# The first attention tiles: small tables for tile 0, masked corners in device memory, earlier key transposes, and the split in front of the reciprocal multiply

## The chip, the cores and the metric

The kernel runs on one core of a Trainium2 chip. The metric is the time of one execution on the device in microseconds (us). TensorE (PE) multiplies matrices and transposes, VectorE (DVE), ScalarE (ACT) and GpSimd (POOL) do the elementwise work, and SyncE (SP) issues nearly all DMAs. Each engine works through its own list of instructions in order; semaphores order the engines among each other.

## The reference

One layer for 1024 prompt frames and 64 sample frames, width 1024. A combined projection gives two attention branches, gates and indexer values. Branch A keeps the best 256 keys per query (by an indexer) and attends over these; branch B attends over the own chunk of 64 and the two before. Both normalise queries and keys by head and add a relative-position bias.

```python
logits = einsum('nqcgd,nqkcd->nqcgk', qg, ks) * HEAD_DIM ** -0.5 + bias    # A; only selected, admissible keys
probs  = softmax(where(valid, logits, NEG))
p      = exp(logits - m); o = einsum(p, v) / (p.sum() + exp(sink - m))     # B; window of whole chunks, sinks
o_a = (att_a * silu(z_a)) @ w_oa ; o_b = (att_b * silu(z_b)) @ w_ob
y   = x + gate * ((sigmoid(g_a) * o_a + sigmoid(g_b) * o_b) @ w_out)
```

A key is admissible if its chunk of 64 is not later than the query's. So in the diagonal block of 128 by 128 the first 64 queries must not see the last 64 keys: one masked corner per tile. Outputs are also the normalised keys, the values and the updated caches.

## The kernel before

The tokens are nine tiles: 0 to 7 of 128 prompt frames, 8 the sample. The kernel has four stages: (1) modulation, norm and transposes of x; (2) projection in 99 pieces (NP), each a product over eight blocks of the contraction in three fp32r matmuls, while VectorE selects the top keys and writes MASK (0 or 1e30); (3) attention; (4) the two output products. The projected q, k and v go to device memory (snat), as do the gates (gz).

Attention is a list of units: per tile eight heads of branch A, then eight of branch B, so 16 units (steps s) a tile; each engine has a loop over s with its own offsets. Per unit u, TensorE computes the negated logits (L1870; for A also a small matmul that adds MASK, L1874), VectorE adds the negated bias and takes the row minimum (L1550), ScalarE takes the exponential (L1255), TensorE transposes the probabilities (L1806), VectorE or ScalarE copies them out of PSUM (t_evac, L544 and L549), and TensorE multiplies with the values (L1896). The biases are tables laid out in device memory by then (btad for A, btbd for B, 128 x 8 heads x keys). Tile 0 has a table of its own for A (BT0) and values for A (VA0). VectorE writes 1e30 into two corners of BTB at s = 6 (L1517, L1518), after the loads of BTB and VB.

The next tile is prepared meanwhile. SP loads QKV at step 16(tt-1) - 7 (L787). POOL multiplies by the norm's weights (L964) and by the reciprocal root (L972) at - 5, and at SPLIT_AT splits q and k into a high and a low part (L981 to L993). TensorE transposes the queries at steps + 9 to + 12 and the keys at + 13 and + 14 (L1829, Q and K in TP). The keys of the sample's cache take the same way in between: ScalarE and POOL split one block of them at steps 32, 48, ... (KSC, L1278, L1009), and TensorE transposes it six steps later.

The end of a group g (a branch of a tile) takes four steps. VectorE multiplies the result with the gate (L1533; the gate is loaded by SP into ATS, L795). The reciprocals of the sums are transposed and go to device memory and back as a broadcast (rdd, RB: L800, L808). POOL multiplies with them (L1004, eight steps after the group's end), and SP stores it (attd, L828). There are two buffers ATS, so a gate load waits for the store of the group two before. SP's list runs in the order of s: gate load, reciprocals, and for the next tile QKV come behind the store of the group before.

## Time and profile before

| | us |
|---|---|
| runs, median of 3 (lowest to highest) | 1006.3 (1005.08 to 1006.81) |
| profiled execution, span from first to last instruction | 1006.1 |
| PE busy | 954.1 (95%) |
| DVE busy | 662.4 (66%) |
| ACT busy | 395.6 (39%) |
| POOL busy | 371.7 (37%) |

The profiled execution shows no time of its own beside the span. Attention runs from about 562 to 803 us of the span, tile 1 from 582.9, tile 2 from 602.2. A row of a timeline has the start, the duration, engine, line, operation, what is written from what, and in brackets how long the engine stood idle before and what ended it.

### The profile page before, as it was taken

The numbers are of one execution on the slowest core, as the hardware profiler recorded it, in microseconds if no ns is written. First come the engines' busy times: TensorE is split into PE (matmuls) and PEld (weight loads), VectorE is DVE, ScalarE is ACT, GpSimd is POOL, SyncE is SP. The second block draws the span as 40 slices with busy tenths as digits, with TensorE's granted clock in tenths as the row PEclk, the third lists the DMA queues.
The fourth block names the chain that finished last, engine by engine and source line by source line (L and its number), as shares of the span: only waits on it lengthen the run. The fifth ranks groups of instructions, "written<-read, shape, count | busy, mean of one in ns | idle before, by whom it ended". The sixth has DMA issues, their size and how long they took to land.

```text
span 1006.1 us, 17578 instructions
## 1 busy us (share of the span) xinstructions
PE 954.1 (95%) x6441; PEld 851.9 (85%) x6455; DVE 662.4 (66%) x1378; ACT 395.6 (39%) x1175; POOL 371.7 (37%) x417
## 2 busy tenths in 40 slices
PE   4859999999999999999999898999999899999998
PEld 2558887878789999999999776787778599999998
DVE  6563365999999999999981475766665763431121
ACT  5674566444432322121211465676665632212100
POOL 0261113212242533131224386766640135536342
PEclk9989999999999999999999789999999999999999
DMA  9830013643462323232231844333315655524342
GB/s 326 304 78 25 24 37 107 226 166 94 127 218 66 108 76 115 74 112 79 66 136 49 254 119 130 118 120 109 106 47 158 194 154 177 161 74 153 110 131 75
DMA packets 110907, 125.87 MB, mean 125 GB/s; under 512 B 10969, under 2 KB 88153, under 8 KB 110698
## 3 DMA queue, kind: packets, MB, share of 16 engines
q1 hardware_dynamic: 100418, 113.77, 36.3%
q10 hardware_dynamic: 10408, 11.01, 3.6%
q8 instruction: 52, 0.85, 0.4%
q14 instruction: 29, 0.24, 0.1%
HBM read 94.96 MB, written 35.75 MB: 130 GB/s over the span
## 4 chain that ended last, share of the span: by engine, by line
PE 82%; issue 4%; DMA 4%; POOL 3%; DVE 3%; ACT 3%; SPq 1%; ACTq 0%; POOLq 0%; DVEq 0%
PE PS L1623 20%; PE PS L1625 19%; PE PS L1624 19%; PE PS L1870 6%; PE PS L1896 6%; PE PS L1806 4%; PE PS L1720 2%; PE PS L1829 2%; POOL YO L1035 1%; PE PS L1874 1%; PE PS L1684 1%; DMA out_y_prompt<-YO 1%; DMA XN<-in_x_prompt 1%; PE PS L1632 1%; DMA VB<-snat 1%
## 5 line engine op out<-in xcount | busy, mean ns | idle before, releaser
L1623 PE MATMUL PS<-HH,WH 128*128 128x384 f32 (+1 forms) x576 | 188.8, 328 | 0.0
L1625 PE MATMUL PS<-HH,WL 128*128 128x384 f32 (+1 forms) x576 | 187.9, 326 | 0.0
L1624 PE MATMUL PS<-HL,WH 128*128 128x384 f32 (+1 forms) x576 | 187.7, 326 | 0.0
L1449 DVE MAX8 M<-SC 128x8 f32<-128x384 f32 (+3 forms) x210 | 174.8, 870 | 11.6 <-DVE SC L1454 11.0
L1454 DVE MATCH_REPLACE8 SC<-M,SC 128x384 f32<-128x384 f32 (+3 forms) x210 | 179.9, 863 | 0.0
L908 POOL TENSOR_TENSOR WL<-RAW,WH 128x512 fp32r<-128x512 f32 x72 | 94.0, 1310 | 180.9 <-ACT WH L1054 180.9
L1623 PE MATMUL PS<-WH,HH 128*128 128x512 f32 (+3 forms) x288 | 110.1, 382 | 8.8 <-DVE HL L1393 8.7
L1623 PEld LDWEIGHTS PS<-HH,WH 128*128 128x128 f32 x576 | 108.1, 188 | 3.8 <-issue 3.7
L1624 PE MATMUL PS<-WL,HH 128*128 128x512 f32 (+3 forms) x288 | 108.4, 376 | 0.0
L1625 PE MATMUL PS<-WH,HL 128*128 128x512 f32 (+3 forms) x288 | 108.2, 376 | 0.0
L1624 PEld LDWEIGHTS PS<-HL,WH 128*128 128x128 f32 x576 | 108.1, 188 | 0.0
L1625 PEld LDWEIGHTS PS<-HH,WL 128*128 128x128 f32 x576 | 108.1, 188 | 0.0
L1255 ACT ACTIVATE PB<-PB,NM 128x256 f32<-128x256 f32 (+9 forms) x136 | 86.2, 634 | 24.1 <-DVE NM L1550 23.1
L1181 ACT ACTIVATE STG<-PS 128x384 f32<-128x384 f32 (+1 forms) x48 | 22.7, 474 | 155.2 <-PE PS L1625 155.2
L1623 PE MATMUL PS<-UH,MH 128*128 128x256 f32 x256 | 72.6, 283 | 0.0
L1624 PE MATMUL PS<-UL,MH 128*128 128x256 f32 x256 | 72.5, 283 | 0.0
L1625 PE MATMUL PS<-UH,ML 128*128 128x256 f32 x256 | 72.3, 282 | 0.0
L1623 PEld LDWEIGHTS PS<-WH,HH 128*128 128x128 f32 (+1 forms) x288 | 53.8, 187 | 19.9 <-POOL WL L908 8.8
L1550 DVE CUSTOM_DVE_ANT_0 PB<-PS,BTA 128x256 f32<-128x256 f32 (+6 forms) x56 | 46.1, 823 | 33.9 <-PE PS L1874 22.3
L1806 PE MATMUL PS<-IDF,PB 128*128 128x128 f32 (+1 forms) x436 | 66.1, 280 | 0.8 <-ACT PT L549 0.7
L1623 PE MATMUL PS<-ZH,WOH 128*128 128x384 f32 (+1 forms) x192 | 63.3, 330 | 1.9 <-POOL WOL L1021 1.9
L1625 PE MATMUL PS<-ZH,WOL 128*128 128x384 f32 (+1 forms) x192 | 63.0, 328 | 0.0
(216 smaller groups left out, 1939.9 us busy)
## 6 DMA issues: line engine op xcount, KB each, us to landing
RAW<-in_w_all SPq DMA_DIRECT2D x72, 256.0 KB, 2.7
gz<-STG SPq DMA_DIRECT2D x48, 192.0 KB, 1.8
WADA<-in_w_ada SPq DMA_DIRECT2D x16, 512.0 KB, 11.8
snat<-STG SPq DMA_DIRECT2D x24, 256.0 KB, 2.0
QKV<-snat SPq DMA_DIRECT2D x8, 768.0 KB, 4.8
GT<-gz SPq DMA_DIRECT2D x32, 192.0 KB, 2.5
XN<-in_x_prompt SPq DMA_DIRECT2D x8, 512.0 KB, 6.2
btad<-bvd ACTq DMA_DIRECT2D x4, 1024.0 KB
```

Source lines behind the costliest of these rows:

```text
L908: nc.gpsimd.tensor_tensor(WL[c % 2][:, k, 0:cw], raw, WH[c % 2][:, k, 0:cw].bitcast(F32), ALU.subtract).then_inc(lo_done, 1)
L1181: nc.scalar.activation(STG[:, q % 3, 0:gn], bank(pbank(p))[:, 0:gn], ACT.Sigmoid).then_inc(piece_ev, 1)
L1255: nc.scalar.activation(PB[u % NPB][0:r, 0:nk], PB[u % NPB][0:r, 0:nk], ACT.Exp, scale=-1.0, bias=NM[0:r, br, h:h + 1], accum_out=DEN[0:r, ...
L1449: V.max(M8[0:r, a, :], w).then_inc(sel_step, 1)
L1454: V.match_replace(w, M8[0:r, a, :], w, TAKEN).then_inc(sel_step, 1)
L1550: V.tensor_tensor_reduce(out=PB[u % NPB][0:r, 0:nk], in0=v, in1=bias, scale=1.0, scalar=init, op0=ALU.add, op1=ALU.min, accum_out=NM[0:r, ...
L1623: T.matmul(out, wh, mh, start=first, stop=False)
L1624: T.matmul(out, wh, ml, start=False, stop=False)
L1625: return T.matmul(out, wl, mh, start=False, stop=last)
L1806: last = T.transpose(out[0:m, c:c + r], PB[v % NPB][0:r, 128 * b:128 * b + m], IDF[0:r, 0:r])
L1870: last = T.matmul(out, q, keys[:, kv, part, k0 + b:k0 + b + m], start=(part == 0), stop=(part == 1 and br == 1))
L1896: last = T.matmul(PS[half, 7, 128 * h:128 * h + r], v, PT[PSLOT[u + kv] % 3][0:m, p_col(u + kv, b):p_col(u + kv, b) + r], start=(b == 0), ...
```

## The change

Tile 0 gets tables of its own for branch B too (BB0, VB0), loaded with BT0 during the last projection chunk. POOL fills a tile NEGT with 1e30, and SP stores it into the masked corners of btad and btbd in device memory, so tables loaded later have it; VectorE's two writes into BTB go, and tiles 0 and 1 leave the MASK matmul out. The K transposes of tile 0 go between the halves of the last projection piece; their copies out of PSUM wait for its end, since the key tables lie over the activations that it reads. The big tables are loaded in another order with semaphores of their own, and the sample's caches (CK, VAS, VBS) at step 14. Constants for the sample are prepared before the last selection. SPLIT_AT goes from 2 to 0: in POOL's loop the split stands before the reciprocal multiply and the cache keys' low part of the same step. Small edits not shown: buffer PB 4 changes places with the later ones, semaphores of the last stage are shared, two waits are added ahead of loads or writes into reused space.

```diff
+        SINKP = at("SINKP", [128, 4], F32, XB + 22784)
+        NSINKP = at("NSINKP", [128, 4], F32, XB + 22816)
         BT0 = at("BT0", [128, 8, 128], F32, WB + 65536)
         VA0 = at("VA0", [128, 128], F32, SCB + 18432)
+        VB0 = at("VB0", [128, 128], F32, SCB + 17920)
+        BB0 = [at(f"BB0{i}", [128, 4, 128], F32, SCB + 10240 + 4096 * i) for i in range(2)]
+        NEGT = at("NEGT", [128, 8, CHUNK], F32, XB + 18432)
         KTB = at("KTB", [128, 2, 2, SEQ], F32R, 102400)
...
-        assert all(TQ[n][1] == ("Q", 0, n) for n in range(EARLY_T))
+        EARLY_T = 6
+        assert [x for _, x in TQ[:EARLY_T]] == [("Q", 0, n) for n in range(4)] + [("K", 0, n) for n in range(2)]
         PREP0 = {16 * (tt - 1): tt for tt in range(NT)}
         CACHE_STEP = {16 * (2 + i): i for i in range(5)}
-        LOAD_AT, NORM_AT, SPLIT_AT = -7, -5, 2
+        LOAD_AT, NORM_AT, SPLIT_AT = -7, -5, 0
         RD_AT, FIN_AT = ({GEND[g] + d: g for g in range(2 * NT)} for d in (1, 4))
...
+                elif x[1] == 0:
+                    eng.wait_ge(piece_pe, NP)
+                    dst = (KTB if x[2] else KTA)[:, :, :, tcols(0)]
...
                         sp.dma_start(dst, src).then_inc(copy_out, 16)
+                if c == NCH - 1 and j == 1:
+                    sp.wait_ge(bias_out, 16 * 5)
+                    sp.wait_ge(neg_set, 1)
+                    sp.dma_start(btad[0:CHUNK, :, 960:1024], NEGT[0:CHUNK, :, :]).then_inc(neg_out, 16)
+                    sp.dma_start(btbd[0:CHUNK, :, 192:256], NEGT[0:CHUNK, :, :]).then_inc(neg_out, 16)
+                    sp.dma_start(btbd[CHUNK:128, :, 0:64], NEGT[CHUNK:128, :, :]).then_inc(neg_out, 16)
                 if c == NCH - 1 and j == 9:
-                    sp.wait_ge(bias_out, 16 * 5)
+                    sp.wait_ge(neg_out, 48)
                     sp.wait_ge(lo_done, KD * NCH)
                     sp.dma_start(BT0[:], btad[:, :, 896:1024]).then_inc(kva_in, 16)
                     sp.wait_ge(mask_done, NT)
                     sp.dma_start(VA0[:], snat[0:128, 640:768]).then_inc(kva_in, 16)
+                    for i in range(2):
+                        sp.dma_start(BB0[i][:], btbd[:, 4 * i:4 * i + 4, 128:256]).then_inc(kva_in, 16)
+                    sp.dma_start(VB0[:], snat[0:128, 1408:1536]).then_inc(vb0_in, 16)
                 if c == NCH - 1 and j == 8:
                     sp.wait_ge(xn4_ready, 1)
...
 
-            sp.dma_start(BTB[:], btbd).then_inc(kvb_in, 16)
-            sp.dma_start(VB[:], vp[:, :, 1408:1536]).then_inc(kvb_in, 16)
-            sp.dma_start(BTA[:, :, 768:1024], btad[:, :, 768:1024]).then_inc(kvc_in, 16)
-            sp.dma_start(VA[:], vp[:, :, 640:768]).then_inc(kvc_in, 16)
-            for dst, src in ((CK[:, 0:4, :], t["cache_ak"].rearrange("(n p) c -> p n c", p=128)), (CK[:, 4, :], t["cache_bk"]),
-                             (VAS[:, 0:4, :], t["cache_av"].rearrange("(n p) c -> p n c", p=128)),
-                             (VAS[0:DEC, 4, :], snat[SEQ:TOK, 640:768]),
-                             (VBS[:, 0, :], t["cache_bv"]), (VBS[0:DEC, 1, :], snat[SEQ:TOK, 1408:1536])):
-                sp.dma_start(dst, src).then_inc(rest_in, 16)
+            sp.dma_start(BTA[:, :, 768:1024], btad[:, :, 768:1024]).then_inc(bta_in, 16)
+            sp.dma_start(VA[:], vp[:, :, 640:768]).then_inc(va_in, 16)
+            sp.dma_start(BTB[:], btbd).then_inc(btb_in, 16)
+            sp.dma_start(VB[:], vp[:, :, 1408:1536]).then_inc(vb_in, 16)
             for i in range(3):
...
                     sp.dma_start(QKV[0:rows_of(tt), tt % 2, :], snat[tcols(tt), :]).then_inc(qkv_in[tt % 2], 16)
+                if s == 14:
+                    for dst, src in ((CK[:, 0:4, :], t["cache_ak"].rearrange("(n p) c -> p n c", p=128)), (CK[:, 4, :], t["cache_bk"]),
+                                     (VAS[:, 0:4, :], t["cache_av"].rearrange("(n p) c -> p n c", p=128)),
+                                     (VAS[0:DEC, 4, :], snat[SEQ:TOK, 640:768]),
+                                     (VBS[:, 0, :], t["cache_bv"]), (VBS[0:DEC, 1, :], snat[SEQ:TOK, 1408:1536])):
+                        sp.dma_start(dst, src).then_inc(rest_in, 16)
                 if s in ZT_AT:
                     g = ZT_AT[s]
...
+            nc.gpsimd.memset(NEGT[:], NEG_BIG).then_inc(neg_set, 1)
             pool.wait_ge(rms_ready, 1)
...
+                    act.wait_ge(pv_pe, 8)
                 if s == NU:
...
+            for i in range(2):
+                V.tensor_copy(IDP[:, i, :], IDF[0:DEC, 0:DEC])
+                half = slice(DEC * i, DEC * (i + 1))
+                V.tensor_copy(SINKP[half, :], SINK[half, :].rearrange("p (a b) -> p a b", b=2)[:, :, i])
+                link(V.tensor_scalar(NSINKP[half, :], SINK[half, :].rearrange("p (a b) -> p a b", b=2)[:, :, i], -1.0, None, ALU.mult))
...
-                    dve.wait_ge(kva_in, 32)
-                    for i in range(3):
+                    dve.wait_ge(kva_in, 64)
+                    for i in range(2):
                         dve.wait_ge(stg_out[i], 16 * NST[i])
                     dve.wait_ge(mask_done, NT)
-                if s == 6:
-                    dve.wait_ge(kvb_in, 32)
-
-                    for i in range(2):
-                        V.tensor_copy(IDP[:, i, :], IDF[0:DEC, 0:DEC])
-                        half = slice(DEC * i, DEC * (i + 1))
-                        V.tensor_copy(SINKP[half, :], SINK[half, :].rearrange("p (a b) -> p a b", b=2)[:, :, i])
-                        V.tensor_scalar(NSINKP[half, :], SINK[half, :].rearrange("p (a b) -> p a b", b=2)[:, :, i], -1.0, None, ALU.mult)
-                    V.memset(BTB[0:CHUNK, :, 192:256], NEG_BIG)
-                    link(V.memset(BTB[CHUNK:128, :, 0:64], NEG_BIG))
-                if s == 16:
-                    dve.wait_ge(kvc_in, 32)
-                if s % 16 == 0 and 32 <= s < U8:
-                    dve.wait_ge(bta_in, 16 * (s // 16 - 1))
+                if s == 4:
+                    dve.wait_ge(stg_out[2], 16 * NST[2])
+                if s == 24:
+                    dve.wait_ge(btb_in, 16)
+                if s % 16 == 0 and 16 <= s < U8:
+                    dve.wait_ge(bta_in, 16 * (s // 16))
                 if s == U8:
                     dve.wait_ge(btp_in[0], 32)
...
+                        bias = BTBP[:, h, :] if tt == SAMPLE else BTB[:, h, j0:j0 + nk] if tt else BB0[h // 4][:, h % 4, :]
                         init = (NSINKP if tt == SAMPLE else NSINK)[:, h:h + 1]
                     dve.wait_ge(qk_pe, u + 1)
...
-                piece(p)
+                if p == NP - 1:
+                    piece(p, (0, 1))
+                    for n in (4, 5):
+                        transposes(TQ[n][1])
+                    piece(p, (2, 3))
+                else:
+                    piece(p)
                 if p in GATE_AT:
                     ada_gate(GATE_AT[p])
                 for n in {NP - 4: (0, 1), NP - 2: (2, 3)}.get(p, ()):
                     transposes(TQ[n][1])
 
-            pe.wait_ge(piece_ev, NP)
             pe.wait_ge(mask_done, NT)
             for s in range(S0, S1):
-                if s == 0:
-                    pe.wait_ge(kva_in, 32)
-                if s == 8:
-                    pe.wait_ge(kvb_in, 32)
-                if s == 16:
-                    pe.wait_ge(kvc_in, 32)
+                if s < 2 and s >= 0:
+                    pe.wait_ge(piece_ev, NP - 2 * (1 - s))
+                if s == 5:
+                    pe.wait_ge(kva_in, 64)
+                if s == 13:
+                    pe.wait_ge(vb0_in, 16)
+                if s == 21:
+                    pe.wait_ge(va_in, 16)
+                if s == 29:
+                    pe.wait_ge(vb_in, 16)
                 if s == 32:
                     pe.wait_ge(rest_in, 96)
                 if 0 <= s < NU:
@@ -1868,8 +1895,8 @@
                         out = PS[:, 2 * (u % 2) + b // 512, 0:m]
                         for part in range(2):
                             last = T.matmul(out, q, keys[:, kv, part, k0 + b:k0 + b + m],
-                                            start=(part == 0), stop=(part == 1 and br == 1))
-                        if br == 0:
+                                            start=(part == 0), stop=(part == 1 and (br == 1 or tt < 2)))
+                        if br == 0 and tt >= 2:
                             r = rows_of(tt)
                             last = T.matmul(out, ident, MASK[0:r, MOFF[tt] + b:MOFF[tt] + b + m], start=False, stop=True)
...
-                                v = VBS[0:m, b, half] if tt == SAMPLE else VB[0:m, max(tt - 1, 0) + b, half]
+                                v = VBS[0:m, b, half] if tt == SAMPLE else VB[0:m, tt - 1 + b, half] if tt else VB0[:, half]
                             last = T.matmul(PS[half, 7, 128 * h:128 * h + r], v, PT[PSLOT[u + kv] % 3][0:m, p_col(u + kv, b):p_col(u + kv, b) + r],
```

## Rows read from the trace of the kernel before

**Rows 1.** The page, part 4: the chain that ended last, by engine.
```profile
PE 82%; issue 4%; DMA 4%; POOL 3%; DVE 3%; ACT 3%; SPq 1%; ACTq 0%; POOLq 0%; DVEq 0%
```
**Rows 2.** Stretches: each engine's busy us (instructions), TensorE's granted clock, DMA share, GB/s.
```profile
564.00:568.00 4.00, 3.85 (x22) 3.20 (x21) 1.62 (x9) 2.38 (x12) 3.92 (x6) 0.55 1.05 350
568.00:572.00 4.00, 1.84 (x11) 1.31 (x10) 3.04 (x12) 1.15 (x5) 1.50 (x4) 0.50 1.11 325
...
620.00:624.00 4.00, 4.00 (x34) 3.53 (x33) 2.46 (x7) 2.27 (x7) 3.23 (x4) 0.70 0.34 96
...
664.00:668.00 4.00, 4.00 (x43) 3.36 (x43) 2.67 (x7) 2.81 (x6) 2.82 (x3) 1.00 0.62 224
```
**Rows 3.** Timeline of TensorE, tiles 0 and 1: start, us, operation, idle before and releaser.
```profile
560.82 0.89 PE L1829 MATMUL PS<-IDR,KS 128*128 128x128 f32 x8 [0.53 <-ACT STG L1181]
...
571.34 0.66 PE L1870 MATMUL PS<-KTB,QT 128*128 128x128 f32 x2 [2.06 <-DVE NM L1550]
...
586.22 0.28 PE L1874 MATMUL PS<-MASK,IDB 128*128 128x256 bf16 x1
```
**Rows 4.** Timeline of ScalarE after the last projection piece.
```profile
560.67 0.58 ACT L558 CAST QT<-PS 128x512 fp32r<-128x512 f32 x1
561.75 0.59 ACT L581 CAST KTB<-PS 128x512 fp32r<-128x512 f32 x1 [0.50 <-PE PS L1829]
```
**Rows 5.** Timeline of VectorE, tiles 0 and 1.
```profile
568.02 0.29 DVE L1513 CAST IDP<-IDF 64x64 bf16<-64x64 f32 x1 [1.59 <-DMA VB<-snat]
...
570.89 0.29 DVE L1550 CUSTOM_DVE_ANT_0 PB<-PS,BT 128x128 f32<-128x128 f32 x1
...
597.58 0.69 DVE L1533 TENSOR_TENSOR ATS<-PS,ATS 128x512 f32<-128x512 f32 x1
```
**Rows 6.** Timeline of SP's DMA issues: start, us spent issuing, line, tiles.
```profile
561.16 0.43 SPq L746 DMA_DIRECT2D BTB<-btbd  x1
...
573.54 0.50 SPq L787 DMA_DIRECT2D QKV<-snat  x1
...
585.43 0.39 SPq L828 DMA_DIRECT2D attd<-ATS  x1
...
587.77 0.36 SPq L795 DMA_DIRECT2D ATS<-gz  x1
...
592.67 0.58 SPq L787 DMA_DIRECT2D QKV<-snat  x1
```
**Rows 7.** Timeline of POOL, tile 2's preparation and the start of tile 3's.
```profile
578.42 3.34 POOL L964 TENSOR_TENSOR XG<-QKV,GAM 128x512 f32<-128x512 f32 x4 [8.92 <-DMA QKV<-snat]
...
584.13 1.28 POOL L1004 TENSOR_TENSOR ATS<-ATS,RB 128x512 f32<-128x512 f32 x1
585.36 1.05 POOL L981 TENSOR_TENSOR QS<-XG,RYQ 128x512 fp32r<-128x512 f32 x1
...
591.38 1.71 POOL L993 TENSOR_TENSOR KS<-XNB,KS 128x128 fp32r<-128x128 f32 x4
...
597.25 3.35 POOL L964 TENSOR_TENSOR XG<-QKV,GAM 128x512 f32<-128x512 f32 x4 [0.45 <-DMA QKV<-snat]
...
608.77 0.88 POOL L1009 TENSOR_TENSOR KSC<-CK,KSC 128x128 fp32r<-128x128 f32 x2
```
**Rows 8.** Timeline of TensorE: transposes of cache keys (KSC), first of tile 3's queries (QS).
```profile
611.13 0.53 PE L1829 MATMUL PS<-IDR,KSC 128*128 128x128 f32 x4
...
617.46 0.51 PE L1829 MATMUL PS<-IDR,QS 128*128 128x128 f32 x4 [2.74 <-POOL KS L993]
...
638.35 0.54 PE L1829 MATMUL PS<-IDR,KSC 128*128 128x128 f32 x4
...
664.44 0.54 PE L1829 MATMUL PS<-IDR,KSC 128*128 128x128 f32 x4
...
693.90 0.54 PE L1829 MATMUL PS<-IDR,KSC 128*128 128x128 f32 x4
```
**Rows 9.** DMA issues by line: count, KB of one, median us from issue to landing.
```profile
ATS<-gz SPq DMA_DIRECT2D x16, 256.0 KB, 3.0
```

More of the change, by code:

```diff
@@ L172, in build_program @@
         BTBP = at("BTBP", [128, 4, WIN + DEC], F32, 121856)
-        IDP = at("IDP", [DEC, 2, DEC], BF16, 66560)
-        SINKP = at("SINKP", [128, 4], F32, 66816)
-        NSINKP = at("NSINKP", [128, 4], F32, 66848)
+        IDP = at("IDP", [DEC, 2, DEC], BF16, XB + 22528)
+        SINKP = at("SINKP", [128, 4], F32, XB + 22784)
+        NSINKP = at("NSINKP", [128, 4], F32, XB + 22816)
         BT0 = at("BT0", [128, 8, 128], F32, WB + 65536)
         VA0 = at("VA0", [128, 128], F32, SCB + 18432)
+        VB0 = at("VB0", [128, 128], F32, SCB + 17920)
+        BB0 = [at(f"BB0{i}", [128, 4, 128], F32, SCB + 10240 + 4096 * i) for i in range(2)]
+        NEGT = at("NEGT", [128, 8, CHUNK], F32, XB + 18432)
         KTB = at("KTB", [128, 2, 2, SEQ], F32R, 102400)
@@ L292, in build_program @@
         stg_out = [sem(f"stg_out{i}") for i in range(3)]
+        neg_set = sem("neg_set")
+        neg_out = sem("neg_out")
         kva_in = sem("kva_in")
-        kvb_in = sem("kvb_in")
-        kvc_in = sem("kvc_in")
+        vb0_in = sem("vb0_in")
+        va_in = sem("va_in")
+        btb_in = sem("btb_in")
+        vb_in = sem("vb_in")
         rest_in = sem("rest_in")
@@ L342, in build_program @@
         u_lo = sem("u_lo")
-        xr_in = [sem(f"xr_in{i}") for i in range(3)]
         y_pe = sem("y_pe")
@@ L348, in build_program @@
         y_up = sem("y_up")
-        y_out = [sem(f"y_out{i}") for i in range(3)]
         SOFF = {}
@@ L777, in _ @@
                     sp.wait_ge(exp_done, NU)
+                    sp.wait_ge(sink_sum, NT)
                     g_load(0)
@@ L1543, in _ @@
                         j0 = 128 if tt == 0 else 0
-                        bias = BTBP[:, h, :] if tt == SAMPLE else BTB[:, h, j0:j0 + nk]
+                        bias = BTBP[:, h, :] if tt == SAMPLE else BTB[:, h, j0:j0 + nk] if tt else BB0[h // 4][:, h % 4, :]
                         init = (NSINKP if tt == SAMPLE else NSINK)[:, h:h + 1]
```

13 lines of the change are left out of this document (6 added, 7 removed).

## The prediction

> **What bounds the kernel now.** I read the page first: TensorE holds 82% of the chain that ended last [rows 1]. So the kernel is bound by TensorE except where TensorE stands still, and the question is where it does. The view of stretches shows two such places near the change. At the start of attention (564 to 572 us) the granted clock falls to 0.55 and 0.50, the lower level of 1.2 GHz, and TensorE is busy for 1.84 of 4 us in the second stretch; around 620 it falls again, to 0.70 of a stretch's mean [rows 2]. From 664 on the stretches are full (4.00 of 4.00). So what is lost before about 664 us stays lost to the end, and what is gained there is kept only if nothing else holds TensorE up before 664.
>
> The timelines by engine say who holds it. At 571.34 TensorE has been idle for 2.06 us for a row minimum of VectorE (NM L1550) [rows 3]; VectorE had stood 1.59 us for the load of VB and then did nine small instructions (IDP, SINKP, NSINKP, two corners of BTB) [rows 5]. The second place is 617.46: 2.74 us for POOL's split of tile 3 (KS L993) [rows 8]. Both are what the change goes for.
>
> The order that matters is a ring through POOL and SP. Per tile, SP stores the attention output of group 0 (attd, L828) only after POOL's reciprocal multiply (ATS L1004); the next gate load (ATS, L795) waits for that store; then come the store and reload of the reciprocals, and only then the next tile's QKV load (L787). In the trace: multiply starts 584.13 and lasts 1.28, store 585.43, gate load 587.77, QKV load 592.67, POOL starts on it at 597.25 [rows 6, 7]. SP follows POOL here to 0.02 us, so the multiply's end sets all of it.
>
> **The change part by part.** All sums are against the profiled span, 1006.1 us; the runs shown have a median of 1006.3, 0.2 more, so nothing of note lies around the span.
>
> *First keys sooner.* The eight K transposes of tile 0 (0.89 us at 560.82) move into the last projection piece. They lengthen that piece by 0.64 to 0.72 (an estimate: their own 0.89 less the pipelined tail), so its end, its evacuation and the four big loads behind it on SP come 0.7 later. What was waited for behind them stays: ScalarE does the evacuation of the piece, then QT (0.58), then KTB (0.59) [rows 4], one after the other, and unit 0 needs KTB. Before, the transposes lay beside QT. From the later end, 0.44 + 0.58 + 0.59 less some overlap gives unit 0 at about 562.6 against 562.5. Bounds: 0.9 gained if the transposes' whole row vanished, 0.7 lost if nothing did. I take 0.
>
> *Small early tables, corners in memory, constants earlier.* The VB wait (1.59) and the nine instructions (568.02 to 570.9) leave VectorE [rows 5]. The six that prepare IDP and SINKP go ahead of the last selection rounds, far from TensorE's needs; the corners become one POOL memset and three stores during the last projection chunk, some 25 us before they are needed. The 256 KB x2 and 64 KB loads go out with BT0 beside the projection. If that cover failed, unit 0 would wait by the length of a load, 3 to 4 us; I put it at nothing. The removed stall is worth TensorE's idle 2.06 at least and VectorE's 4.4 at most. Next late is TensorE itself, full at the half clock, so I take 2.1.
>
> *Masks left out in tiles 0 and 1.* Sixteen small matmuls go (0.28 us for one of 256 columns [rows 3]). Bounds: nothing, where VectorE is waited for, and 16 x 0.28 = 4.5. They are pipelined and the next matmul starts about 0.12 behind one, so I take 1.4. The lead is then 2.1 + 1.4 = 3.5 us by unit 25 (bounds 0 to 9).
>
> *Load order.* Ahead of tile 2's QKV load SP now issues BTA, VA, BTB and VB (3072 KB as before), while CK, VAS and VBS (704 KB by their shapes) go behind it. Before, the first table was issued at 561.16, SP got to the QKV load at 573.54 and POOL started at 578.42 [rows 6, 7]. The DMAs move 325 to 350 GB/s in these stretches [rows 2], so 0.72 MB less is 2.2 us sooner; the later end of the last piece takes back 0.7. POOL starts on tile 2 at 578.4 - 2.2 + 0.7 = 576.9. Bounds: 579.1 (only the delay) and 572.0: SP itself reaches this load 5.5 us sooner, and if it landed as soon after its issue as before it would be 572.9, less at most 1. I take 576.9, because that data still queues behind the same 3 MB.
> The Trainium skill (DMA: Bandwidth & Descriptors, Anatomy of one DMA) fits a transfer at 2.0 us plus bytes over 436 GB/s, a fit made for POOL's own queue. By it the 4.26 MB up to this load would take 11.8 us from 561.9, an estimate of 573.7, and the final sum below would be 3.2 smaller; the 325 to 350 GB/s of the trace do not bear out that rate, and the sum goes without it.
>
> *Split ahead of the reciprocal multiply.* This is the part that decides. The split moves from step 2 to step 0 of each 16, and in POOL's loop the split stands before the multiply of the same step and before the cache keys' low part (KSC L1009). So multiply and KSC now queue behind 7.73 us of split (585.36 to 593.09, the last row's end) [rows 7]. Who waits for the multiply: SP's store at the next step, and behind it the gate load, the reciprocals of group 1 and the next QKV load. Who waits for KSC: TensorE's transposes of the cache keys at step 38, in program order three steps before tile 3's own query transposes.
>
> The ring before: end of multiply to QKV issue 592.67 - 585.41 = 7.26; to POOL's start 4.58; the two norm steps 5.71 (578.42 to 584.13); multiply 1.28; together 18.9 us, with the split beside SP's part. After: the split is inside, 18.9 + 7.73 = 26.6 us per tile. TensorE needs, from cache transposes to cache transposes, 27.2 for the first turn (of which 2.74 idle, and about 1 at a lower clock), 26.1 for the second and 29.5 for the third [rows 8]. So a ring that had some 5 us of air per tile now has none until tile 4 or 5.
>
> In absolute times. First multiply ends at 576.9 + 5.71 + 7.73 + 1.28 = 591.6 (before 585.4).
> - Gate load of group 2 goes at 591.6 + 2.36 = 594.0 and lands 3.0 later (median of that load [rows 9]), 597.0. VectorE needs it for the multiply that it did at 597.58 [rows 5]. With the lead of 3.5 it would be there at 594; so it waits 3 us and the lead is gone.
> - Second multiply ends at 591.6 + 26.6 = 618.2, KSC 0.88 later [rows 7], 619.1. The cache transposes were at 611.13: 8.0 us late.
> - Third: 618.2 + 26.6 = 644.8, KSC 645.7; before 638.35: 7.3 late. TensorE by itself would come at 619.1 + 23.4 = 642.5, some 1.5 more with the half clock after the long idle, so it waits again.
> - Fourth: 671.4, KSC 672.3; before 664.44: 7.9 late. TensorE by itself: 645.7 + 26.1 = 671.8.
> - Fifth: 698.9 against 672.3 + 29.5 = 701.8 by TensorE itself. From here TensorE is the bound, and the delay stays.
>
> So the sum is not the lead minus something; the lead is swallowed, and the ring sets +7.9. I add 0.8 for later QKV loads that may land slower beside other traffic and for half clock after the two short waits (0 to 2). +8.7 on 1006.1 is 1014.8, 1015.0 beside the median of the runs.
>
> **The rivals.**
> 1. *The ring does not bind, and the lead is kept* (not slower). Place: POOL's start on tile 2. All later times go with it one to one, so at 576.9 - 7.9 = 569.0 the fourth KSC is on time. Then the lead of 3.5 and perhaps the 2.74 at 617.46 stay won: 1000 to 1003. For it: SP is free for this load near 568 and the split of tile 3 did stand 4 us behind a multiply that waited for its data. Against: the load itself would have to land a microsecond after its issue, behind 3 MB. Or SP's chain from multiply to QKV load would have to shrink from 7.3 us, which is made of waits for DMAs that the change leaves in place. Chance 0.10.
> 2. *Lead and ring cancel.* POOL starts on tile 2 at 569 to 571, or the ring is 2 to 3 us shorter a turn: 1004 to 1008. For it the same rows as rival 1; against it that both ends of the load's bounds lie above 571. Chance 0.08, of which 0.05 within 0.2%.
> 3. *Worse: the waits cost the clock as well.* TensorE stands about 8 us ahead of the first cache transposes; after the 2.74 us at 617 the trace shows a lower clock (0.70) for one stretch [rows 2, 8]. If each of the three waits costs 1.5 to 2 us more, and QKV loads land 2 us later, the end is 1018 to 1022. Chance 0.10.
> The forecast itself has 0.72, with its own range from 1010.5 (load at the 573 bound, ring 26) to 1018.
>
> **How the numbers follow.** A difference under 0.2%, 2 us, cannot be told from no change here. Slower: forecast, rival 3 and a rest of rival 2, 0.72 + 0.10 + 0.01 = 0.83; same 0.05; faster 0.10 + 0.02 = 0.12. The range of 8 in 10 leaves out rival 1 and the far end of rival 3: 1008 to 1019.5.
>
> **What would show it.** In the changed trace: VectorE without the 4.4 us near step 6, and unit 8 about 2 us sooner; unit 0 within 0.3 of 562.5; POOL on tile 2 at 575 to 578, its first L1004 behind the split, ending near 591.6; SP's first attd store there and not at 585; VectorE's second L1533 no sooner than 597; TensorE idle for several us ahead of the KSC transposes, near 619; steps of about 26.6 us between the L1004 that follow splits; the granted clock low behind these waits. I am wrong if the first L1004 behind the split ends before 586, or if the KSC transposes run at 611 or sooner, or if TensorE still waits for KS L993 and not for KSC.

## The result, and the profile after the change

The changed kernel takes 1021.57 us (median of 4 runs, 1020.52 to 1023.54), the kernel before 1005.72 beside it: ratio 1.0162, 95% interval 1.0144 to 1.0181. The change costs 1.6%. The forecast had the sign and the place right (slower, through the ring of POOL and SP) and the size too small: 1015.0, with a range that ended at 1019.5.

In the profiled execution the span is 1020.3 us, against 1006.1. The device time of that execution is 1022.09, 1.8 above its span, and it is 1.8 to 2.0 above the span in every run since. If it was so for the kernel before too, its profiled execution took some 1007.9 (an estimate, its time is not on record), about 2 more than the median of its own kernel. The prediction had put 0.2 there.

The page's chain of work that ended last has a new member:

```profile
PE 77%; POOL 8%; issue 5%; DMA 3%; DVE 3%; ACT 2%; SPq 1%; ACTq 0%; POOLq 0%; DVEq 0%
```

POOL holds 8% of it where it held 3% [rows 1], TensorE 77% where it held 82%. The stretches say where (columns as in [rows 2]: busy us of PE, PEld, DVE, ACT, POOL; granted clock; DMA share; GB/s):

```profile
564.00:568.00 4.00, 3.39 (x17) 2.59 (x18) 1.85 (x13) 3.09 (x14) 3.67 (x6) 0.66 0.92 261
568.00:572.00 4.00, 3.77 (x23) 3.06 (x22) 1.76 (x10) 1.93 (x8) 0.00 (x0) 0.50 1.06 371
616.00:620.00 4.00, 0.00 (x0) 0.00 (x0) 0.00 (x0) 0.59 (x2) 4.00 (x7) 0.99 0.01 2
620.00:624.00 4.00, 2.39 (x10) 1.71 (x10) 1.21 (x3) 0.00 (x0) 1.47 (x3) 0.50 0.54 141
664.00:668.00 4.00, 4.00 (x34) 3.06 (x32) 3.52 (x8) 2.69 (x7) 3.92 (x5) 1.00 0.26 86
```

Two things are to be seen. The stall at 568 is gone: TensorE is busy for 3.77 of 4 us where it was busy for 1.84 [rows 2]. And there is a far worse one at 616: TensorE does nothing in a whole stretch, POOL all of it, and in the stretch behind it TensorE runs at 0.50, its lower level of 1.2 GHz.

TensorE's timeline, first at the start of attention, then at the transposes of the cache keys (start, us, line, operation, idle before and releaser):

```profile
563.30 0.63 PE L1897 MATMUL PS<-KTA,QT 128*128 128x128 f32 x4 [1.58 <-ACT KTB L589]
...
569.71 0.69 PE L1897 MATMUL PS<-KTB,QT 128*128 128x128 f32 x2
...
621.61 0.72 PE L1847 MATMUL PS<-IDR,KSC 128*128 128x128 f32 x4 [6.14 <-POOL KSC L1029]
...
676.48 0.51 PE L1847 MATMUL PS<-IDR,KSC 128*128 128x128 f32 x4 [0.28 <-POOL KSC L1029]
...
707.80 0.54 PE L1847 MATMUL PS<-IDR,KSC 128*128 128x128 f32 x4
...
739.73 0.54 PE L1847 MATMUL PS<-IDR,KSC 128*128 128x128 f32 x4
```

Unit 8 comes at 569.71 instead of 571.34 with no wait for VectorE. The cache transposes come at 621.61, 649.84, 676.48, 707.80 and 739.73: against [rows 8] 10.5, 11.5, 12.0 and 13.9 later, and 13.9 at the fifth (725.82 before). From there to the end almost nothing more is lost (the span is 14.2 longer). TensorE waits for the low part of the cache keys at the first and the third; the second has no wait in front of it.

SP's issues and POOL's work around tile 2 show how it comes:

```profile
566.57 4.84 SPq L835 DMA_DIRECT2D out_pa_k<-XNB  x1
...
571.94 0.66 SPq L800 DMA_DIRECT2D QKV<-snat  x1
...
594.35 0.38 SPq L847 DMA_DIRECT2D attd<-ATS  x1
596.67 0.37 SPq L814 DMA_DIRECT2D ATS<-gz  x1
...
600.71 0.59 SPq L800 DMA_DIRECT2D QKV<-snat  x1
```

```profile
579.68 3.34 POOL L984 TENSOR_TENSOR XG<-QKV,GAM 128x512 f32<-128x512 f32 x4 [12.01 <-DMA QKV<-snat]
583.10 2.33 POOL L992 TENSOR_TENSOR XNB<-XG,RYQ 128x1280 f32<-128x1280 f32 x1
585.39 1.04 POOL L1001 TENSOR_TENSOR QS<-XG,RYQ 128x512 fp32r<-128x512 f32 x1
...
591.40 1.69 POOL L1013 TENSOR_TENSOR KS<-XNB,KS 128x128 fp32r<-128x128 f32 x4
593.05 1.27 POOL L1024 TENSOR_TENSOR ATS<-ATS,RB 128x512 f32<-128x512 f32 x1
...
606.03 3.34 POOL L984 TENSOR_TENSOR XG<-QKV,GAM 128x512 f32<-128x512 f32 x4 [1.53 <-DMA QKV<-snat]
...
619.39 1.25 POOL L1024 TENSOR_TENSOR ATS<-ATS,RB 128x512 f32<-128x512 f32 x1
620.61 0.86 POOL L1029 TENSOR_TENSOR KSC<-CK,KSC 128x128 fp32r<-128x128 f32 x2
```

Read them in turn: the multiply waits for nothing but the split (585.39 to 593.09) and ends at 594.32 instead of 585.41 [rows 7]; SP's store follows at 594.35, the gate load at 596.67, the next QKV load at 600.71 (592.67 before [rows 6]), POOL's next norm at 606.03 (597.25), its split, the next multiply at 619.39, and behind that the low part of the cache keys, for which TensorE has been standing since about 615.5. The multiplies behind the splits end at 594.32, 620.64, 648.14, 675.50 and 704.57: turns of 26.3, 27.5, 27.4 and 29.1 us.

The forecast has nothing on what shows on VectorE beside POOL (all engines in one timeline):

```profile
636.87 2.33 POOL L992 TENSOR_TENSOR XNB<-XG,RYQ 128x1280 f32<-128x1280 f32 x1
...
637.45 1.78 DVE L1576 TENSOR_TENSOR SD<-NM,SINK 128x8 f32<-128x8 f32 x1
...
639.88 0.70 PE L1923 MATMUL PS<-PT,VB 128*64 128x128 f32 x8 [2.04 <-DVE PT L549]
...
693.28 2.33 POOL L992 TENSOR_TENSOR XNB<-XG,RYQ 128x1280 f32<-128x1280 f32 x1
...
693.59 2.04 DVE L1576 TENSOR_TENSOR SD<-NM,SINK 128x8 f32<-128x8 f32 x1
...
696.29 0.66 PE L1923 MATMUL PS<-PT,VB 128*64 128x128 f32 x8 [2.21 <-DVE PT L549]
```

A sum of 128x8, which takes 0.16 us on tile 3, takes 1.78 and 2.04 us here and ends when POOL's multiply ends (639.20 and 695.61 by start and duration); TensorE waits 2.04 and 2.21 us for the copy behind it. The sum takes 1.88 and 1.38 us on tiles 2 and 5 too.

### The profile page after: what moved, and what is told of

Same layout as the page of the kernel before. It is cut to its first block, busy times and chain, and to the rows that moved or that the text cites. A ratio compares the mean times of both kernels' runs of the same rounds, so it can differ in the third digit from the quotient of the medians.

```text
span 1020.3 us, 17573 instructions
## 1 busy us (share of the span) xinstructions
PE 959.8 (94%) x6439; PEld 855.6 (84%) x6439; DVE 665.7 (65%) x1376; ACT 396.1 (39%) x1175; POOL 373.3 (37%) x418
## 4 chain that ended last, share of the span: by engine, by line
PE 77%; POOL 8%; issue 5%; DMA 3%; DVE 3%; ACT 2%; SPq 1%; ACTq 0%; POOLq 0%; DVEq 0%
PE PS L1641 19%; PE PS L1643 19%; PE PS L1642 19%; PE PS L1923 4%; PE PS L1897 4%; PE PS L1824 3%; PE PS L1738 2%; POOL YO L1055 1%; PE PS L1847 1%; PE PS L1901 1%; POOL XG L984 1%; POOL QS L1009 1%; PE PS L1702 1%; DMA XN<-in_x_prompt 1%; POOL QS L1001 1%
## 5 line engine op out<-in xcount | busy, mean ns | idle before, releaser
L1276 ACT ACTIVATE PB<-PB,NM 128x256 f32<-128x256 f32 (+9 forms) x136 | 86.2, 634 | 27.6 <-DVE NM L1568 26.4
L1824 PE MATMUL PS<-IDF,PB 128*128 128x128 f32 (+1 forms) x436 | 68.3, 287 | 0.7 <-ACT PT L554 0.7
L1897 PE MATMUL PS<-KTA,QT 128*128 128x512 f32 (+3 forms) x192 | 62.4, 430 | 2.1 <-ACT KTB L589 1.6
```

The lines of the kernel that those rows point to most:

```text
L1276: nc.scalar.activation(PB[u % NPB][0:r, 0:nk], PB[u % NPB][0:r, 0:nk], ACT.Exp, scale=-1.0, bias=NM[0:r, br, h:h + 1], accum_out=DEN[0:r, ...
L1824: last = T.transpose(out[0:m, c:c + r], PB[v % NPB][0:r, 128 * b:128 * b + m], IDF[0:r, 0:r])
L1897: last = T.matmul(out, q, keys[:, kv, part, k0 + b:k0 + b + m], start=(part == 0), stop=(part == 1 and (br == 1 or tt < 2)))
```

## Experiments

The theory of the forecast: the split, put ahead of the multiply, lies inside the ring, and the ring sets the pace until tile 5. Rivals: the other parts of the change carry some of the loss; the cache keys' place behind the split carries it, and no ring; POOL's start on tile 2 sets it all; VectorE held up by POOL sets it. All ratios are to the kernel before, run beside each on the same chip. To compare kernels by TensorE's milestones one must know that the whole execution up to the last projection piece shifts by some us: SP's store of that piece was issued at 560.80 in the profile of before, at 562.22 in that of after, and between 560.66 and 563.81 in the others. So the table gives the cache transposes also as time since that store.

| kernel | median us | ratio [95%] | cache transposes 1 to 3 since that store | turns 1-2, 2-3, 3-4 |
|---|---|---|---|---|
| before | 1003.97 to 1005.72 | 1 | 50.3, 77.6, 103.6 | 27.2, 26.1, 29.5 |
| after | 1021.57 | 1.0162 [1.0144, 1.0181] | 59.4, 87.6, 114.3 | 28.2, 26.6, 31.3 |
| splits late again | 1004.68 | 0.9997 [0.9976, 1.0018] | 53.0, 75.8, 101.9 | 22.8, 26.1, 29.5 |
| only the splits early | 1022.68 | 1.0162 [1.0122, 1.0203] | 59.6, 86.7, 114.2 | 27.1, 27.5, 29.4 |
| tile 2's load sooner | 1018.92 | 1.0141 [1.0109, 1.0174] | 56.1, 82.7, 110.0 | 26.6, 27.3, 30.5 |
| cache keys ahead of split | 1018.46 | 1.0157 [1.0107, 1.0208] | 53.2, 80.8, 112.0 | 27.6, 31.2, 29.9 |
| ring cut | 1008.24 | 1.0032 [1.0014, 1.0051] | 53.0, 77.6, 103.7 | 24.6, 26.1, 29.5 |
| ring cut, cache keys ahead of multiply | 1005.20 | 1.0001 [0.9985, 1.0018] | 50.2, 73.6, 99.7 | 23.4, 26.1, 29.5 |
| the same, tile 2's load sooner | 1003.29 | 0.9998 [0.9981, 1.0016] | 49.8, 72.7, 98.8 | 22.8, 26.1, 29.5 |
| splits late, tile 2's load sooner | 1002.95 | 0.9971 [0.9954, 0.9987] | 49.4, 72.2, 98.3 | 22.8, 26.1, 29.5 |
| the same, loads and norms sooner | 1011.36 | 1.0060 [1.0037, 1.0082] | 49.3, 74.7, 106.6 | 25.4, 31.9, 30.5 |
| POOL's multiply in four | 1021.60 | 1.0171 [1.0136, 1.0205] | 60.9, 88.4, 116.0 | 27.5, 27.6, 29.6 |

**One part undone, one part alone.** The whole change with the splits at their old step:

```diff
-        LOAD_AT, NORM_AT, SPLIT_AT = -7, -5, 0
+        LOAD_AT, NORM_AT, SPLIT_AT = -7, -5, 2
```

> The changed kernel with the split back at step 2, behind the reciprocal multiply and the cache keys' low part; everything else of the change stays. Ring theory (the split inside the ring of POOL and SP makes the whole loss): POOL starts tile 2 at 579.7 as in the changed kernel, the first multiply ends at 586.7 instead of 594.3, the cache transposes are on time near 611, and the split of tile 3 ends near 618.6, a little later than before the change, so the lead of the first tiles is spent there: 1003 to 1008 us, 1006 likeliest. Rival (the front of the change loses by itself, by the longer half clock and the later QKV load): above 1012 us.

Measured 1004.68, ratio 0.9997: the loss is gone, and the other parts together are worth nothing that can be told. The cache transposes came at 615.13 and not near 611, with no wait for POOL in front of them (why they are late is taken up below, with the lead of 3.5 us). And the kernel before with this one number changed the other way (2 to 0):

> The kernel before with the split at step 0 and nothing else of the change. Ring theory: POOL starts tile 2 at 578.4, the first multiply behind the split ends at 593.1, the turns are 26.5 to 27.5 us as in the changed kernel, the cache transposes come at 620, 648, 675: 1017 to 1021 us. Rival (the moved split only hurts together with the new load order): under 1010 us.

Measured 1022.68, 1.7 above the range that was expected, ratio 1.0162, the ratio of the whole change. The cache transposes came at 621.78, 648.89 and 676.38. TensorE's timeline in it:

```profile
621.78 0.72 PE L1829 MATMUL PS<-IDR,KSC 128*128 128x128 f32 x4 [7.92 <-POOL KSC L1009]
```

The wait is 7.92 us for the same operation of POOL. So one number carries the loss, and the order of loads, the small tables, the early keys and the masks neither cause it nor soften it by anything that the two intervals let one tell (0.9976 to 1.0018, 1.0122 to 1.0203).

**Tile 2's load sooner.** On the changed kernel, the load at position 3 of the last chunk instead of behind the big tables:

```diff
+                if c == NCH - 1 and j == 3:
+                    sp.wait_ge(xg_ready, 1)
+                    sp.dma_start(QKV[:, 0, :], snat[tcols(2), :]).then_inc(qkv_in[0], 16)
...
-                if tt is not None and tt >= 2:
+                if tt is not None and tt >= 3:
```

> The changed kernel with tile 2's QKV load issued in the last projection chunk, ahead of the big tables. POOL can then norm tile 2 near 568, and the split waits only for the key transposes of tile 1 near 581; the first multiply behind it ends near 590 instead of 594.3. Ring theory: every later turn is 4 us sooner, the end 3 to 5 us sooner than the changed kernel, 1016 to 1019 us, still slower than before. Rival (the late QKV load of tile 2 is the cause): under 1008 us. Rival (it is not in the chain at all): 1021 us.

Measured 1018.92. POOL starts on it 13.6 us sooner, but the second half of its norm only 7.1:

```profile
566.09 3.32 POOL L987 TENSOR_TENSOR XG<-QKV,GAM 128x512 f32<-128x512 f32 x4
576.00 2.33 POOL L995 TENSOR_TENSOR XNB<-XG,RYQ 128x1280 f32<-128x1280 f32 x1 [6.60 <-issue]
...
588.07 1.28 POOL L1027 TENSOR_TENSOR ATS<-ATS,RB 128x512 f32<-128x512 f32 x1
```

The second half overwrites the tile from which SP's key store (out_pa_k) reads, and that store is the one on which SP spent 4.84 us: here it was issued at 565.48 and landed 10.4 us later, and it is now the last to be waited for. Counted from the store of the last piece, the first multiply comes 3.4 us sooner (27.4 against 30.8), and the first, third and fifth cache transposes come 3.3, 4.3 and 5.1 sooner: the ring's turns stay (26.6, 27.3), and what is won at its start is kept. The expectation of the ring holds; the medians differ by 2.7, but the intervals of the two ratios overlap.

**The cache keys' low part ahead of the split**, the six lines moved up in POOL's loop, nothing else:

> The changed kernel with the cache keys' low part ahead of the split of the same step; the reciprocal multiply stays behind the split. If TensorE's loss comes mainly from the cache transposes three steps ahead of the query transposes (KSC queued behind split and multiply), TensorE passes step 38 near 615 and waits at step 41 for the split: 1010 to 1015 us. If the ring alone sets the time, whatever waits for it, nothing is won: 1020 us or more.

Measured 1018.46: a miss, and the more useful one. The first cache transposes do come sooner by 6.2 us since the store (53.2 against 59.4), but now TensorE waits at the next thing that the split makes:

```profile
616.96 0.53 PE L1847 MATMUL PS<-IDR,KSC 128*128 128x128 f32 x4
...
622.31 0.51 PE L1847 MATMUL PS<-IDR,QS 128*128 128x128 f32 x4 [1.76 <-POOL KS L1020]
```

and by the third cache transposes 2.3 us of the 6.2 are left (112.0 against 114.3). The rival that the cache keys' place carries the loss is wrong: the multiplies behind the splits still follow each other every 27.6 to 28.7 us (595.8, 623.4, 652.1, 679.9 their ends), and the time is not told from that of the changed kernel.

**The ring cut.** The load of a tile's projection rows nine steps and its norm four steps sooner (the splits stay early). The norm of a tile then runs while POOL waits for the reciprocals of the second multiply anyway, and the load is long issued, so neither adds to the way from one multiply behind a split to the next:

```diff
-        S0, S1 = -23, NU + 9
+        S0, S1 = -26, NU + 9
...
-        LOAD_AT, NORM_AT, SPLIT_AT = -7, -5, 0
+        LOAD_AT, NORM_AT, SPLIT_AT = -16, -9, 0
```

First with the cache keys' low part also moved, to between split and multiply; the second run leaves it where the change has it:

> The changed kernel with the splits ahead of the reciprocals as they are, but the load of a tile's projection rows nine steps sooner and its norm four steps sooner, and the cache copy's low part between split and reciprocal multiply: the chain from one even multiply to the next (store, gate load, reciprocals, projection load, norm, split, multiply) is cut, because load and norm no longer lie in it. Ring theory: the even multiplies follow each other every 22 to 26 us, as the units allow, instead of 26.3 to 29.1, the transposes of the cache copy come at 611 to 616 and later at the distances of the kernel before (27 to 31), and the time is 1000 to 1007, the loss of 16 gone. Rival (it is POOL's order at each step, split ahead of multiply, that costs, whatever the ring does, or VectorE held by POOL's multiplies): multiplies still 27 to 29 apart, time 1015 to 1022.

Measured 1005.20, ratio 1.0001. The multiplies behind the splits start at 591.74, 612.60 and 634.94: 20.9 and 22.3 us apart, where the changed kernel had 26.3 and 27.5.

> The changed kernel with one thing altered, the loads of a tile's projection rows nine steps and its norm four steps sooner; split ahead of reciprocals and the cache copy's low part behind them, as in the change. Together with the cache copy's move this took away the whole loss (1.0001). Theory ring (load and norm inside the chain of even multiplies is nearly all of it): the even multiplies come every 22 to 26 us on tiles 2 to 4, the cache transposes wait 1 to 2 us at most for the low part, 1.000 to 1.004 of the kernel before, 1004 to 1009. Rival (the cache copy's place behind the multiply carries as much): the transposes still wait 4 us or more at tile 2, ratio 1.006 to 1.015, 1011 to 1020.

Measured 1008.24, ratio 1.0032, as the ring theory has it; TensorE waits 2.65 us, a little more than expected, and once:

```profile
615.07 0.51 PE L1847 MATMUL PS<-IDR,KSC 128*128 128x128 f32 x4 [2.65 <-POOL KSC L1029]
```

So of the 1.62%, cutting the ring takes away about 1.3 and the cache keys' place about 0.3, which shows only once the ring is gone (the intervals of the two runs just meet; in the traces the cache transposes are 2.8 to 4.0 us apart). The split is early and ahead of the multiply in both: its place there costs nothing by itself.

**POOL's multiply in four.** On the changed kernel, L992 as four instructions of five heads:

```diff
-                    nc.gpsimd.tensor_tensor(XNB[0:r, :, :], XG[0:r, :, :],
-                                            RYQ[0:r, 20 * tt:20 * tt + 20].unsqueeze(2).broadcast_to([r, 20, HD]), ALU.mult).then_inc(xn4_ready, 1)
+                    for b in range(4):
+                        last = nc.gpsimd.tensor_tensor(XNB[0:r, 5 * b:5 * b + 5, :], XG[0:r, 5 * b:5 * b + 5, :],
+                                                       RYQ[0:r, 20 * tt + 5 * b:20 * tt + 5 * b + 5].unsqueeze(2).broadcast_to([r, 5, HD]), ALU.mult)
+                    last.then_inc(xn4_ready, 1)
```

> The changed kernel with POOL's one multiply of 128x1280 elements (2.33 us) cut into four of five heads each, the same elements. In the changed kernel VectorE's small sum of 128x8 took 1.88, 1.78 and 2.04 us instead of 0.16 on tiles 2, 4 and 6, and ended when this multiply ended. Theory (an operation of VectorE with two inputs from SBUF waits for the POOL instruction under way): the sum takes at most 0.8 us, TensorE's waits of 2.04 and 2.21 us behind it shrink to about 1, the time falls by 2 to 4 us, to 1017 to 1020. Rival (the coincidence is of starts, or the ring hides it): the sum stays near 1.9 or shrinks without the time moving: 1021 to 1023.

```profile
636.94 2.76 POOL L993 TENSOR_TENSOR XNB<-XG,RYQ 128x320 f32<-128x320 f32 x4
...
637.21 0.48 DVE L1578 TENSOR_TENSOR SD<-NM,SINK 128x8 f32<-128x8 f32 x1
...
638.34 0.66 PE L1925 MATMUL PS<-PT,VB 128*64 128x128 f32 x8 [0.74 <-DVE PT L549]
...
693.93 2.77 POOL L993 TENSOR_TENSOR XNB<-XG,RYQ 128x320 f32<-128x320 f32 x4
...
694.32 0.35 DVE L1578 TENSOR_TENSOR SD<-NM,SINK 128x8 f32<-128x8 f32 x1
...
695.33 0.66 PE L1925 MATMUL PS<-PT,VB 128*64 128x128 f32 x8 [0.53 <-DVE PT L549]
```

The sum takes 0.48 and 0.35 us, TensorE's waits fall from 2.04 and 2.21 to 0.74 and 0.53: VectorE did wait for the POOL instruction under way. The turn from third to fourth cache transposes is 29.6 again, the 29.5 of before, where it was 31.3. But the time, 1021.60, did not move: the four take 0.44 us more (2.77 against 2.33), and that lies in the ring. By the third cache transposes this kernel is 1.7 us later than the changed one (116.0 against 114.3 since the store), close to four times 0.44, and the fourth come at 145.6 in both. So the theory holds for the sum and the waits, and the rival for the time. The Trainium skill (GPSIMD Engine Reference, Specifications) says that POOL shares its interfaces to SBUF with VectorE and that VectorE instructions with two inputs from SBUF contend for them; this sum has two, and the trace agrees with 1.78 to 2.04 us behind one long instruction and 0.35 to 0.48 behind short ones.

**Is there a better kernel?** Three tries, on two questions: what is left at the front, and whether late splits and a cut ring add up.

> The changed kernel with the splits back at their old step (two steps later) and the second tile's projection rows loaded one SP position sooner, ahead of the key store that held SP for 4.84 us. With the splits late the first tiles came out even with the kernel before (0.9997), the next tile's multiplies starting on POOL at 579.3. Theory A (what POOL does on tile 2 sets the pace, and its late load ate the lead of the front): POOL starts tile 2's norm some 10 us sooner, its first gate multiply ends at about 580 instead of 586, the transposes of the cache copy come at about 611 instead of 615, the time is 0.996 to 0.999 of the kernel before (1001 to 1004). Theory B (the units of tile 3 wait for something else, the split of tile 3 by its step, and the half clock until 600): same time as with the splits late alone, 1004 to 1006, the transposes still at 614 to 616.

Measured 1002.95, ratio 0.9971 [0.9954, 0.9987]: 0.3% faster than the kernel before and, by the ratios, 1.9% faster than the changed one; from the splits late alone it is not told (the intervals overlap). The time is theory A's, but its mechanism is not shown. The multiply did not come at 580 (583.97 its start; the norm's second half waited 6.50 us for the key store here too), and the cache transposes came at 613.17, between the two theories. Since the store of the last piece they are 3.6 us sooner than with the splits late alone (49.4 against 53.0), although TensorE stood idle no less on the way (3.3 us against 2.4, from 8 us behind that store on). What differs is its clock (the splits late alone, then this kernel; columns as above):

```profile
568.00:600.00 32.00, 29.77 (x158) 23.66 (x157) 17.25 (x59) 14.50 (x51) 18.18 (x22) 0.51 0.69 216
568.00:600.00 32.00, 28.70 (x183) 23.01 (x183) 17.86 (x66) 16.90 (x61) 20.32 (x27) 0.64 0.74 216
```

The clock is 0.51 of these 32 us there and 0.64 here, with TensorE busy for less of them. That is the half clock of theory B. Whether the earlier load brought the clock back sooner, or the two only went together in this one execution, stays open.

> The changed kernel with loads and norms sooner and the cache copy's low part ahead of the multiply (1.0001 as it stood, POOL starting tile 2 at 578.35), and the second tile's projection load one SP position sooner. If POOL's start on tile 2 is what delays tile 3: first even multiply at about 587 instead of 591.7, cache transposes at 607 to 610 instead of 612.05, 0.995 to 0.998, 1000 to 1003. If not: 612 and 0.998 to 1.002, 1003 to 1007.

Measured 1003.29, ratio 0.9998: the second case. The first multiply started at 589.20 and the cache transposes came at 611.63, hardly sooner, so there POOL's start on tile 2 is not what delays tile 3. Its milestones are within 0.5 us of those of the one above, and the time is not told from the kernel before's. Why it does not show a gain as that one does stays open; the two intervals overlap.

> The changed kernel with the splits at their old step, the second tile's projection load one SP position sooner (these two alone gave 0.9971) and the loads and norms of all tiles sooner as well. If POOL's chain still holds up tiles 2 to 4 with late splits: the cache transposes at 608 to 612 instead of 613.17, 635.98, 662.08, time 0.993 to 0.996, 998 to 1001. If TensorE is the bound from 600 on (19.44 us busy of 20 there): the same as with the two alone, 0.996 to 0.999, 1001 to 1004.

Measured 1011.36, ratio 1.0060: wrong both ways, since two settings that are each harmless are slower together. POOL's timeline shows a ring again:

```profile
582.84 1.27 POOL L1027 TENSOR_TENSOR ATS<-ATS,RB 128x512 f32<-128x512 f32 x1 [2.56 <-DMA RB<-rdd]
584.06 1.04 POOL L1004 TENSOR_TENSOR QS<-XG,RYQ 128x512 fp32r<-128x512 f32 x1
...
591.74 3.34 POOL L987 TENSOR_TENSOR XG<-QKV,GAM 128x512 f32<-128x512 f32 x4
595.16 2.34 POOL L995 TENSOR_TENSOR XNB<-XG,RYQ 128x1280 f32<-128x1280 f32 x1
597.46 1.28 POOL L1027 TENSOR_TENSOR ATS<-ATS,RB 128x512 f32<-128x512 f32 x1
607.98 1.28 POOL L1027 TENSOR_TENSOR ATS<-ATS,RB 128x512 f32<-128x512 f32 x1 [9.25 <-DMA RB<-rdd]
```

With the split two steps later and the norm four sooner, both stand between one multiply and the other (584.06 to 597.50). The next reciprocals wait for that multiply's store and come 9.25 us later, and then split and norm follow again: a ring of 25.9 to 26.6 us (597.46, 623.49, 650.05, 675.99 the starts), by chance the length of the forecast's, made of other parts. TensorE waits 2.34 and 2.87 us for the split in it (at 617.94 and 644.54). No run takes this ring apart again, so that it makes the whole loss is read from the timeline only.

## Why the prediction was right in direction and too small

The mechanism was the one forecast, and three terms of the sum failed: POOL's start on tile 2 was put too early (2.5 us of the loss), the ring's later turns too short (1.7), and the hold of VectorE by POOL at nothing (1.8). One by one:

**The ring: right.** The wait moved as worked out: from POOL's split of tile 3 (2.74 [rows 8]) to the cache keys' low part (6.14), the store followed the multiply at 594.35, the first turn was 26.3 against 26.6, and the clock was at its lower level behind the wait. That the split's place decides, and that the rest of the change neither gains nor loses, is shown by the two experiments on that one number.

**POOL's start on tile 2: 576.9 forecast, 579.68 measured.** This term is 2.8 short: 0.7 because the last piece's store came 1.4 later where I had 0.7 (with only the splits early, where the last piece is that of the kernel before, it came at 562.20 as well, so that the longer piece did this is not shown), and the rest for the load. The load order did bring the issue forward, from 12.7 to 9.7 us after the last piece's store (573.54 - 560.80, 571.94 - 562.22). But POOL started 17.6 us after it before and 17.5 after the change. The 2.2 us for 0.72 MB less were worth nothing: the load landed later after its issue (7.7 us to POOL's start, against 4.9). The 4.84 us that SP spent on the key store ahead of it are not the reason. With the ring cut and the cache keys ahead of the multiply, this load stands ahead of the key store in SP's list:

```profile
566.05 5.33 SPq L800 DMA_DIRECT2D QKV<-snat  x1
...
578.35 3.32 POOL L984 TENSOR_TENSOR XG<-QKV,GAM 128x512 f32<-128x512 f32 x4 [11.01 <-DMA QKV<-snat]
```

That is 4.2 and 16.5 us after the last piece's store: issued 5.5 us sooner, the load brought POOL's start forward by 1.0. Only ahead of the tables was it there by the time POOL came to it (566.09, 5.4 us after the store, in the kernel with tile 2's load sooner). The measured start is 0.6 beyond the upper bound that I had given, 579.1; taking a value inside the bounds by the rate of transfer was the fault. The fit that I quoted from the Trainium skill (DMA: Bandwidth & Descriptors, Anatomy of one DMA) gave 573.7 and is further off still. The first multiply's end (594.32 against 591.6) and the first cache transposes (621.61 against 619.1) carry it on unchanged.

**The ring's later turns: 26.6 forecast, 27.5, 27.4 and 29.1 measured.** From SP's issue of a QKV load to POOL's start it took 4.6 us in the row of before; here 5.3, 5.7, 5.6 and 6.0 (600.71 to 606.03, and 627.74, 655.21, 683.88 to 633.43, 660.79, 689.85). From the multiply's end to that issue it took 6.4, 7.1, 7.1 and 8.4 against 7.3. The page's median from issue to landing of these loads is 5.6, where it was 4.8. I had 0.8 in all for this; it cost 1.7 by the third cache transposes (676.48 against 672.3, less the 2.5 already there), for which TensorE waits for the ring again. The second, at 649.84, are not the ring's, as the forecast had it: the low part was done at 648.96, and TensorE, which had stood 2.04 us behind VectorE's sum on the way, came to it 0.9 later.

**From the third cache transposes on: "TensorE is the bound, and the delay stays".** Wrong by 1.8 us, the turn of 31.3 instead of 29.5: VectorE's sum behind POOL's multiply, and TensorE's wait of 2.21 behind it. That the four shorter instructions brought this turn back to 29.6 shows it; and with only the splits early, where the sum of that turn took 0.17 us, it is 29.4. The forecast had no term for what POOL does to VectorE when the two meet elsewhere than before; the kernel before had such meetings too, but of 1.03 and 0.68 us.

**The time around the span.** The forecast of 1014.8 for the span compares with 1020.3, which is 5.5 short: 2.5 from the start, 1.7 from the turns and 1.8 from the sum make 6.0, less the 0.8 that I had added, and 0.3 that I can't place. The time is 6.6 short: the changed kernel's median lies 1.3 above its profiled span, and I had 0.2. And if the profiled execution of before was some 2 us above its own median, as estimated above, that is why the traces show 14.2 us of loss and the medians 15.9.

**First keys at nothing: nearly right.** Unit 0 came at 563.30, 0.8 later, where I had allowed 0.3, and 0.7 as the worst; measured from the last piece's store it is 1.1 us behind it instead of 1.7, while the piece itself is longer by the transposes.

**Lead of 3.5, swallowed: it was, but not as I had it, so this was luck.** Unit 8 stood 7.5 us behind the store instead of 10.5, so 3.0 were won, and the gate multiply of VectorE that stood at 597.58 [rows 5] came at 601.56. But it did not wait for the gate load issued at 596.67: it has no wait in front of it, and with the splits late again, where that load was issued 8.1 us sooner (588.61), it came at 601.48. (With only the splits early the forecast's wait is there, 1.44 us at 600.06.) What the rows show instead is TensorE's clock (before, then after):

```profile
568.00:600.00 32.00, 28.12 (x204) 22.59 (x202) 22.46 (x77) 17.33 (x61) 20.05 (x26) 0.74 0.65 191
568.00:600.00 32.00, 29.57 (x157) 23.53 (x157) 16.83 (x59) 14.50 (x51) 14.48 (x18) 0.51 0.57 175
```

The granted clock of these 32 us is 0.51 after the change and 0.74 before. With the splits late again it is 0.51 too, and there the first cache transposes come 2.7 us later since the store than before (53.0 against 50.3), with no wait for POOL. The forecast had no term for this. In the changed kernel it is hidden, because TensorE then stands for 6.14 us. What keeps the clock down is open: with the ring cut and the cache keys ahead of the multiply, whose tables and masks are the same, it is 0.73.

**Rivals.** Rivals 1 and 2 fell: POOL's start was not at 569 to 571. Rival 3, with a chance of 0.10, gave 1018 to 1022 and is nearest to what was measured; its slower loads are there (0.7 to 1.4 us a load, 1.7 in all), its 1.5 to 2 us for the clock at each wait hardly: after 6.14 us of standing the clock was 0.50 and 0.66 for two stretches, but at most 0.9 us of this came through to the second cache transposes and none to the third, where the ring sets the time again, and the two later waits for the cache keys were 0 and 0.28 us.

## What to carry to other kernels

When an operation is moved ahead of another on the same engine, look for the ring: what waits for the one behind, through which DMAs, and whether that leads back to the operation moved; the length of the ring against the consumer's own pace per tile gave the sign and more than half of the loss here, and cutting the ring (an earlier load, an earlier norm) made the same move harmless. Two moves that are harmless alone can close a ring together, so each pair wants its own sum. Where a load's data stood behind 3 MB that were issued before it, issuing it 3 or 5.5 us sooner brought it 0.1 or 1.0 us sooner; only the kernels that issued it ahead of them had it in time. And a time that comes out as forecast does not show the cause: look in the rows for the wait that was forecast.

## What the hardware showed that was not expected

- A VectorE sum of 128x8 from two SBUF tiles was held for 1.38 to 2.04 us, until POOL's multiply of 2.33 us had ended; behind POOL instructions of a quarter of the elements it took 0.16 to 0.48 us on tiles 2 to 6 (and 0.92 twice later, where it met POOL instructions of the split).
- Cut in four, POOL's multiply of 128x1280 cost 2.77 us instead of 2.33, so some 0.15 us for each further instruction.
- SP spent 4.84 us issuing one small store when four big loads stood in its queue; that store's later issues in the same kernel took 0.35 to 0.59 us. In the kernels with the ring cut, where the QKV load stood in that place, it was the QKV load that took 4.75 and 5.33 us, so behind these four loads it is the place in the queue and not the transfer that decides. In the kernel before, with the tables in another order, the longest issue there was that of the fourth load (VA, 3.45 us).
